# Skipping unused overflow blocks and casting twenty experts' weights ahead, in an eight-core hybrid layer

## What is computed

```python
def hierarchical_moe(h, w_group, b_group, w_router, b_router, w_up, w_down):
    ...
    g_prob = jax.nn.softmax((t @ w_group + b_group).astype(jnp.float32), axis=-1)   # (n, N_GROUPS)
    p_g, g_idx = lax.top_k(g_prob, 1)                                                # (n, 1)
    ...
    top_p, top_i = lax.top_k(jax.nn.softmax(e_sel, axis=-1), TOP_K)
    ...
    for e in range(N_EXPERTS):
        a, u = jnp.split(t @ w_up[e], 2, axis=-1)
        y = y + combine[:, e:e + 1] * ((jax.nn.silu(a) * u) @ w_down[e])
```

## Time and profile before

| | us |
|---|---|
| median of 3 runs | 1048.96 |
| lowest, highest | 1013.27, 1062.71 |
| profiled execution, time of the run | 1017.43 |
| its span, slowest core (7) | 1015.7 |
| spans of the eight cores | 981.9 to 1015.7 |

### The profile page before, as it was taken

How to read it: one execution, slowest core, us unless ns; L and a number is a source line. 1 busy time by engine, 2 the same in 40 slices (tenths; PEclk the granted TensorE clock), 3 DMA queues, 4 the chain that set the end, 5 groups by cost and what they waited for, 6 DMA issues and landing times. The chain is left out here.

```text
span 1015.7 us, 16550 instructions; the slowest of 8 cores (981.9 to 1015.7 us)
## 1 busy us (share of the span) xinstructions
PE 879.5 (87%) x6340; PEld 501.3 (49%) x6340; DVE 562.8 (55%) x1060; ACT 425.3 (42%) x847; POOL 331.4 (33%) x341
## 2 busy tenths in 40 slices
PE   5788999998999999999996278859898998889694
PEld 2344553444544444444544156546666666667342
DVE  1548747879246346677757843333443344435287
ACT  2335325544555644334324013323343343644395
POOL 2112302444224320000010236654566566565200
PEclk9988999989999999999996579989999899999798
DMA  8995897240106016012029878999999989898485
GB/s 154 206 222 136 144 172 133 43 83 2 42 5 203 2 29 158 22 41 95 32 83 169 161 140 150 188 198 194 207 181 176 194 159 212 146 194 162 145 333 206
DMA packets 41811, 140.19 MB, mean 138 GB/s; under 512 B 14704, under 2 KB 19440, under 8 KB 34563
## 3 DMA queue, kind: packets, MB, share of 16 engines
q0 software_dynamic: 24256, 95.29, 51.8%
q1 hardware_dynamic: 17476, 43.84, 12.8%
HBM read 253.66 MB, written 37.22 MB: 286 GB/s over the span
## 5 line engine op out<-in xcount | busy, mean ns | idle before, releaser
L492 PE MATMUL ps<-sb 128*128 128x512 bf16 (+9 forms) x5248 | 824.3, 312 | 94.0 <-DVE sb L525 22.7
L492 PEld LDWEIGHTS ps<-sb 128*128 128x128 bf16 (+4 forms) x5248 | 433.6, 102 | 450.4 <-issue 109.6
L505 ACT ACTIVATE sb<-ps 128x512 bf16<-128x512 f32 (+3 forms) x599 | 320.2, 583 | 444.7 <-PE ps L492 332.9
L510 DVE TENSOR_TENSOR sb<-ps,sb 128x256 bf16<-128x256 f32 (+4 forms) x222 | 96.9, 443 | 162.1 <-PE ps L492 84.1
L1215 POOL DMA_INDIRECT sb<-hd,sb x94 | 100.8, 1072 | 93.6 <-PE ps L492 39.9
L525 DVE COPY sb<-ps 128x1024 bf16<-128x1024 bf16 (+4 forms) x109 | 73.3, 676 | 99.9 <-PE ps L1227 44.6
L807 POOL TENSOR_TENSOR sb<-sb 128x512 bf16<-128x512 bf16 x60 | 74.3, 1242 | 141.7 <-ACT sb L505 134.6
L1265 POOL DMA_INDIRECT yd<-sb x94 | 99.1, 1054 | 47.9 <-ACT sb L505 23.6
L522 DVE SCALAR_TENSOR_TENSOR sb<-sb 128x1024 f32<-128x1024 f32 (+5 forms) x92 | 97.7, 1072 | 1.6
L507 ACT ACTIVATE sb<-sb 128x1024 bf16<-128x1024 f32 x50 | 52.6, 1052 | 76.5 <-DVE sb L510 45.1
L522 DVE SCALAR_TENSOR_TENSOR sb<-sb,ps 128x512 f32<-128x512 f32 x68 | 46.5, 685 | 59.2 <-PE ps L492 50.8
(11 more groups left out here) (44 smaller groups left out, 165.3 us busy)
## 6 DMA issues: line engine op xcount, KB each, us to landing
sb<-wex POOLq DMA_DIRECT2D x47, 1536.0 KB
sb<-x SPq DMA_DIRECT2D x32, 512.0 KB, 9.7
sb<-wad POOLq DMA_DIRECT2D x12, 1024.0 KB, 16.4
sb<-wsl POOLq DMA_DIRECT2D x8, 1024.0 KB, 20.7
sb<-yd SPq DMA_DIRECT2D x16, 512.0 KB, 5.9
out<-sb SPq DMA_DIRECT2D x16, 512.0 KB, 3.2
sb<-wo SPq DMA_DIRECT2D x8, 512.0 KB, 4.4
hd<-sb SPq DMA_DIRECT2D x16, 256.0 KB, 3.0
```

The lines of the kernel that those rows point to most:

```text
L492: ins = e.matmul(o, lhsT=l, rhs=r, start=s0, stop=s1)
L505: S.op("act", lambda e: e.activation(out=out, in_=in_, func=func, scale=scale), reads=[in_] + list(extra), writes=w)
L510: S.op(eng, lambda e: e.tensor_tensor(out=out, in0=a, in1=b, op=op), reads=[a, b], writes=[out])
```

## The change

Three things. First, five overflow blocks (KDYN) stay among the static ones, and the other ten go into a region of their own behind all others. PE, ACT, DVE and POOL load a flag (whether overflow block 5 is in use) and jump over the region where it is 0. The planner orders the part ahead, the region and the part behind apart; what follows waits for a join on POOL instead of the region's operations. The semaphores of the region are separate.

Second, the weights of twenty experts (7 to 9, 11 to 13, 15 to 18, 20 to 22, 24 to 26 and 28 to 31) are cast to bf16 into a tensor wbf in device memory, in forty halves on POOL's queue that are woven among the mixer's steps, each waiting for the half two before it. The block's `W` then loads wbf without a cast.

Third, `fold_step`'s loads of wo and `x1_load` of chunks 0 to 2 move from SP's queue to POOL's.

```diff
+KDYN = 5
+NPRE = 20
+PREK = (7, 9, 9, 9, 6)
...
+                    emit_ops(parts[0])
+                    if parts[1]:
+                        v_ = eng.value_load(self.flag, min_val=0, max_val=1)
+                        with eng.If(v_ > 0):
+                            emit_ops(parts[1])
+                            if e == "pool":
+                                for k, v in rfinal:
+                                    eng.wait_ge(sems[k], v)
+                    emit_ops(parts[2])
...
+    wbf_d = nc.dram_tensor("wbf", [NPRE, 128, 6144], BF16).ap()
...
+        def pre_step():
+            h = _ph[0]
+            if h >= 2 * NPRE:
+                return
+            _ph[0] += 1
+            q, p = divmod(h, 2)
+            o_ = wbf_d[q, p * 64:(p + 1) * 64, :]; i_ = wex_d[prel[q], p * 64:(p + 1) * 64, :]
+            S.op("pool", lambda e: e.dma_start(out=o_, in_=i_), reads=[("wbf", h - 2)] if h >= 2 else [("xl", 17)], writes=[("wbf", h)], dma=("wbf", h % 2), cost=6.95)
...
-        weave(main, att_steps((0, 1)))
+        weave(mix(main, PREK[0]), att_steps((0, 1)))
...
-                sdma(s_, wo_d[h, :, k2 * 1024:(k2 + 1) * 1024], ("wst", q % 2))
+                gdma(s_, wo_d[h, :, k2 * 1024:(k2 + 1) * 1024], ("wst", q % 2))
...
-                sdma(x1t(t), x_d[t * 128:(t + 1) * 128, :].rearrange("p (a n) -> p a n", n=256), ("x1", t), also=[("x1", t)])
+                (sdma if c == 3 else gdma)(x1t(t), x_d[t * 128:(t + 1) * 128, :].rearrange("p (a n) -> p a n", n=256), ("x1", t), also=[("x1", t)])
...
-                gdma(r_, wex_d[n], ("wr", i % NRING), after)
+                if n in pre:
+                    S.op("pool", lambda e: e.dma_start(out=r_, in_=wbf_d[pre[n]]), reads=[("wbf", 2 * pre[n]), ("wbf", 2 * pre[n] + 1)] + list(after), writes=[r_],
+                         dma=("wr", i % NRING), cost=4.8)
+                else:
+                    gdma(r_, wex_d[n], ("wr", i % NRING), after)
...
+        run_items(0, NA)
+        for e_ in ("pe", "act", "dve", "pool"):
+            S.op(e_, lambda e: e.nop(), reads=[eidi], writes=[("br", e_)], cost=0.05)
+        r0 = len(S.ops)
+        for i in range(NRING):
+            W(NA + i)
+            if i < 4:
+                G(NA + i)
+        T(NA)
+        run_items(NA, NI)
+        r1 = len(S.ops)
+        join = S.op("pool", lambda e: e.nop(), writes=[("join", 0)], cost=0.05)
+        S.region = (r0, r1, join)
+        S.flag = eidi[0:1, NDYN + KDYN:NDYN + KDYN + 1]
```

More of the change, by code:

```diff
@@ L44, in __init__ @@
         self.cache = {}
+        self.region = None
     def _dsem(self, key):
@@ L144, in order, with _run @@
         n = len(ops)
[L145 to L148, removed]
-            for d in o["deps"]:
-                succ[d].append(i)
+        lo, hi, join = self.region
+        for i in range(hi, n):
+            d = ops[i]["deps"]
+            if i != join and any(lo <= k < hi for k in d):
+                ops[i]["deps"] = set(k for k in d if not lo <= k < hi) | {join}
+        ops[join]["deps"] = set(k for k in ops[join]["deps"] if not lo <= k < hi)
+        st = self._run(list(range(lo)), window, lat, None)
+        order = list(st["out"])
+        order += self._run(list(range(lo, hi)), window, lat, None)["out"]
+        st["out"] = []
+        order += self._run(list(range(hi, n)), window, lat, st)["out"]
+        pos = {i: k for k, i in enumerate(order)}
+        self.model = max(o["end"] for i, o in enumerate(ops) if not lo <= i < hi)
+        self.ops = [ops[i] for i in order]
+        for o in self.ops:
+            o["deps"] = set(pos[d] for d in o["deps"])
+        self.region = (lo, hi, pos[join])
+    def _run(self, ids, window, lat, st):
+        ops = self.ops
+        n = len(ids)
+        succ = {i: [] for i in ids}
+        left = {}
+        at = {}
+        inside = set(ids)
+        for i in ids:
+            o = ops[i]
+            left[i] = 0
+            at[i] = 0.0
+            for d in o["deps"]:
+                if d in inside:
+                    left[i] += 1
+                    succ[d].append(i)
+                elif st is not None:
+                    at[i] = max(at[i], ops[d]["end"] + lat)
         ready = {e: [] for e in self.ENGS}
-        free = {e: 0.0 for e in self.ENGS}
-        at = [0.0] * n
         ev = []
-        rings = {"pool": [[], 0.8], "sp": [[], 0.2]}
-        tprev = 0.0
+        if st is None:
+            st = dict(free={e: 0.0 for e in self.ENGS}, rings={"pool": [[], 0.8], "sp": [[], 0.2]}, t=0.0, out=[])
+        free, rings, out = st["free"], st["rings"], st["out"]
+        tprev = st["t"]
         oldest = 0
+        where = {i: k for k, i in enumerate(ids)}
         done = [False] * n
-        out = []
         def finish(i, end):
@@ L241, in order @@
         assert len(out) == n
[L242 to L246, removed]
+        st["t"] = tprev
+        return st
     def emit(self):
@@ L258, in emit @@
                 o["sig"] = True
-        cnt = {e: 0 for e in self.ENGS}
-        dcnt = {}
-        for o in ops:
+        lo, hi, join = self.region
+        cnt = {}
+        for i, o in enumerate(ops):
+            r = "r" if lo <= i < hi else "m"
             if not o["sig"]:
@@ L292, in emit @@
                 waits.append((k, v))
[L293 to L305, removed]
+            prog[e][0 if i < lo else 1 if i < hi else 2].append((waits, o))
+        final = [(k, v) for k, v in cnt.items() if k[0] == "m" and k != ("m", "e", "sp")]
+        rfinal = [(k, v) for k, v in cnt.items() if k[0] == "r"]
+        assert not prog["sp"][1]
+        self.stats = dict(n_ops=len(ops), cnt=cnt)
+        sems = {k: self.esem[k[2]] if k[:2] == ("m", "e") else self._dsem(k) for k in cnt}
         nc = self.nc
@@ L959, in build_program @@
         se, sd = 8, 0
[L960 to L961 removed]
+        while se < NE or sd < KDYN:
+            if sd < KDYN and (sd + 1) * (NE - 8) <= (se - 8 + 1) * KDYN + KDYN:
                 items.append(("d", sd)); sd += 1
```

117 lines of the change are left out of this document (67 added, 50 removed).

## The result

The changed kernel takes 976.43 us (median of four runs, 966.86 to 994.16), the kernel before, run beside it, 1031.12 (four runs, 1011.01 to 1062.71). The ratio is 0.9602, with an interval of 0.9503 to 0.9701: 4.0% faster, where 940 of 1017.4 would have been 7.6%. The ratio is taken over undisturbed executions alone; in the others the cores of one die show a lower granted clock and take longer. The profiled execution took 977.85 us; its slowest core is core 3.

A forecast was written before the change was run, and what follows sets the result against it. PE was taken to bound the mixer, with DMA often idle; PE and late weights (DMA) the expert blocks. 1017.4 - 98 (blocks) + 15 (stores) + 5 (branch and join) = 939.4, say 940 us; range 905 to 988.

The forecast's parts named there:

- What the branch takes away: Overflow blocks beyond five: no core takes the branch, 37 blocks run and ten are skipped, with almost no DMA traffic saved.
- The blocks: Expert blocks: 37 at 7.0 us instead of 47 at 7.6, 98 us less; 117 and 76 at the bounds.
- The stores of hd: SP's stores of normalised tiles, 400 to 531 us: slow landings stall DVE and PE for one group, 15 us; bounds 0 and 60.
- its upper bound of 6.2 us: Casts during the mixer: half an expert's cast takes 4.2 us by reads alone, 6.2 if written bytes count as well.
- The stores starve: Rival: all three groups of tiles stand the full time for hd stores, 60 us instead of 15, giving 985 us; chance 15%.
- I cost them at nothing too: Mixer: wo loads and twelve x tiles on POOL's queue arrive up to 12 us later behind halves, charged at nothing.
- The masks themselves: Attention masks on POOL, 162.0 to 368.1 us: 22 halves among them, one in 9.4 us, cost nothing.
- Branch, join and tail: Behind the blocks: jumps, POOL join and ACT's later diagonal scalings cost 5 us; bounds 0 and 10.
- the mostly vanished wait for wex: Sign of being right: DVE's wait for expert weights in the blocks, 17.8 us before, mostly gone.
- the busy POOL queue: Sign of being right: POOL's queue busy from 150 to 500 us, during the mixer.
- an hd landing well above 3 us: Sign of being right: median landing of hd stores well above 3 us, with DVE waiting around 400 to 430 us.
- the first up projection: Start of the expert blocks: near 610 us if right; after 640 was a sign of being wrong.

The follow-up runs named there:

- e1: Changed kernel with the branch alone: no casts ahead, wo and x loads back on SP's queue; ratio 0.9939 to the kernel before, median 1008.5 us.
- e2: Changed kernel with the casts and moved loads alone: all 15 overflow blocks static, no branch; ratio 1.0303 to the kernel before, median 1044.03 us.
- e3: Changed kernel with each cast half written in 256 pieces of 3 KB instead of 32 of 24.6 KB; ratio 0.9377 to the kernel before, median 949.61 us.
- e7: Changed kernel with four buffers instead of two for normalised tiles 0 to 11, long pieces kept; ratio 0.9448 to the kernel before, median 956.5 us.
- e9: e8 with the first four expert loads in three column slices each; ratio 0.9291 to the kernel before, median 940.4 us.
- e8: Changed kernel with e3's small pieces and four buffers for tiles 0 to 11 together; median 949.91 us, runs too far apart for an interval.
- e10: e8 again, in more executions, beside e9; ratio 0.9363 to the kernel before, median 950.08 us.
- e6: Changed kernel with wo and x loads back on SP's queue, halves in long pieces; ratio 1.0472 to the kernel before, median 1055.37 us.

## Why the prediction was wrong

**What the branch takes away** came as forecast. No core took the branch; 560 matmuls and ten blocks are gone.

**The blocks** held within the bounds: 98 us forecast, at 7.0 us a block; 89.7 on the slowest cores, at 267.4 / 37 = 7.2 us, and 89.3 in the mean, at 6.9. e1 and e2 show that the working rested rightly on both limits: with PE's alone lifted the blocks gain 3 us, with the DMA engines' alone 17.

**The stores of hd are the step that failed:** "I take 15 us, one group, since rows 8 show the long landing only under load and fourteen halves do not fill these 131 us." They did fill them: from 400 to 531 us the DMA engines are busy 0.98. The working set 87 us of halves against 131, and left out that 0.20 of these 131 us, 26, were taken already. A half also lasts longer than its upper bound of 6.2 us: issues behind one another are about 7 us apart (442.52 and 449.61), which makes some 99 us of fourteen. And the halves are no short burst: each waits for the half two before it, and the last was issued at 516.73, so that they met all the stores up to there. So more than one group of tiles stalled. On core 3 the chain has stores of 20.0, 30.0 and 29.7 us in the first two groups, on the other cores the third group stalled too, and the stores took 31.1 us more in the mean, where I had 15. The long landing itself was in the earlier trace rows, with expert loads of 128x6144 under way, and the halves' pieces are twice as long. "The stores starve" is the rival that came true, at 15% where the forecast had 53%: its mechanism, long pieces on the other queue and two buffers, is the one that e3, e7 and e9 show. That its 985 us lie 7 from the profiled 977.85 is partly luck: it had 60 us in the stores, where these cost about half, and nothing ahead of them. The profiled time lies near the upper end of the range of 905 to 988, which was drawn to take this rival in.

How a store's time hangs on the other queue's pieces shows in two pairs of runs: with halves in pieces an eighth as long the stores' extra 31.1 us fell to 9.9 (e3), and with the first expert loads in thirds POOL's wait, 20 to 25 us in e8 and e10, fell to 4.4 to 6.7 (e9). This agrees with the rule that I had put behind the rival, from the Trainium skill (DMA: Bandwidth & Descriptors, Queues, rings and completion order), that each DMA engine takes turns between queues packet by packet. By it the landing was to exceed 29.6 us, and it did: 30.0 is the longest on the chain, and 46.7 the longest of all on core 3. How large a turn is no run shows: a store did not shorten in step with the pieces.

**"I cost them at nothing too"**, of the wo loads and x tiles, failed as well; the first store came 10.8 us later in the mean. The chain has three loads of wo with 16.5, 16.3 and 21.2 us and one of wad with 19.6, each behind halves, while DVE waits 11.3 us for wo. My 12 us for each group of tiles was given as the price if the cover was gone, and not put into the sum. But DVE's wait for wo grew only from 4.7 to 8.0 us in the mean of the cores, so that it shows a third of the 10.8. The last masks began 9.0 us later in the mean already. Where the rest is lost is open. The masks themselves cost next to nothing, as forecast: on core 3 POOL stood before them for ACT above all (81.3 us), and PE waited 2.0 us for them.

**Branch, join and tail** were oversized: 5 us forecast, 0.6 in the mean and 1.9 on the slowest cores. The compare and jump on core 3, of PE (PEldq is its sequencer) and of POOL (ns, start):

```profile
L351 PEldq COMPARE_BRANCH  x1: 4976/4976/4976, 909.1 to 909.1; - x1
...
L351 POOLq COMPARE_BRANCH  x1: 50/50/50, 911.0 to 911.0; - x1
```

On PE it lasts 3.4 to 5.0 us over the eight cores, on DVE, ACT and POOL 45 to 72 ns. PE's agrees with the stall for a taken branch to a target outside the loaded window, from the Trainium skill (Runtime: NRT & Kernel Launch, Instruction fetch mechanics), and a 16 KB packet of an instruction queue runs within it (from 911.62 us on core 3). That the jump would not hide was wrong: it ends at 914.07, before the load of yd is issued at 914.94, and PE's first sum waits for that load until 918.73. The landing (3.63 us) and the load of yd (3.65) together are about as long as in the earlier trace rows.

The sum with what was measured: 1015.7 - 89.7 + 48.3 + 1.9 = 976.2 us, where the last two stood at 15 and 5.

Of the signs that I had named, the mostly vanished wait for wex (on the four cores that had waited most for it), the busy POOL queue, an hd landing well above 3 us and DVE's wait for hd, from 418 to 430 us, came; the first up projection at 643.84, behind 640, was the one named as wrong, and it was.

## What to carry to other kernels

Idle DMA engines under a busy PE are not free: a background transfer in long pieces lengthens the short transfers that another queue has on the path, here a store from 2 to 20 us; in pieces an eighth as long, with the same bytes, to 12. Cut the background's pieces, and give short stores enough buffers to be late, before moving work into such a gap. Where two limits of a stage lie a few per cent apart, lift both in one change and expect little of either alone (here 3 and 17 us of 89).

## What the hardware showed beyond expectation

A transfer from device memory to device memory that reads 1.57 MB of f32 and writes 0.79 MB of bf16 came about every 7 us with the engines full, more than read and written bytes together had given by the loads' rate (6.2). The length of its pieces did not change that much: POOL waited 134.4 us for halves with long pieces and 127.8 with pieces an eighth as long (both core 3), while the stores beside them took 21.2 us less. On SP's queue a load of wo beside long halves made DVE wait 57.0 us at the longest (e6); on POOL's own queue, in line behind them, the three loads of wo on the chain landed 16 to 21 us after their issue. And a jump over code that is skipped is not equally cheap on every engine: it took 3.4 to 5.0 us on PE, which skips 560 matmuls, and under 0.1 us on the other three; why they differ was not tested.
